# Expert rows turned in 32x32 blocks by VectorE instead of whole by TensorE, and the memory attention's value product with its operands swapped

## What is computed

```python
def memory_attention(q, mem, g_mem, w_kv):          # 4 heads of 64, 256 memory rows for each sequence
    ...
    p = jax.nn.softmax(scores, axis=-1)
    o = jnp.einsum('bhsm,bmhd->bshd', p, v)
...
def expert_choice(xn, w_router, w_gate, w_up, w_down):
    aff = jax.nn.softmax((xt @ w_router), axis=-1)   # 16 experts
    g, idx = lax.top_k(aff.T, cap)                   # each expert takes 256 + 128 rows
    xe = xt[idx]
    hdn = silu(einsum('ecd,edf->ecf', xe, w_gate)) * einsum('ecd,edf->ecf', xe, w_up)
    ye = einsum('ecf,efd->ecd', hdn, w_down) * g[..., None]
    y = zeros_like(xt).at[idx.reshape(-1)].add(ye.reshape(-1, D))
...
    o = concat([rmsnorm(o_a), rmsnorm(o_b), rmsnorm(o_c)])   # o_c is the memory attention's
    x = x + o @ w_out
    x = x + expert_choice(rmsnorm(x, g_ffn), ...)
    return rmsnorm(x, g_final)
```

## Time and profile before

| | |
|---|---|
| median of 3 runs | 3428.23 us (3425.49 to 3431.06) |
| the profiled execution | 3429.16 us |
| its span, first to last instruction | 3427.4 us |
| TensorE busy | 3269.1 us, 95% |
| VectorE, ScalarE, GpSimd busy | 1618.2, 1440.3, 543.9 us |
| mean granted TensorE clock | 0.973 |

### The profile page before, as it was taken

How to read it: one execution, slowest core, us unless ns; L and a number is a source line. 1 busy time by engine, 2 the same in 40 slices (tenths; PEclk the granted TensorE clock), 3 DMA queues, 4 the chain that set the end, 5 groups by cost and what they waited for, 6 DMA issues and landing times. The chain is left out here.

```text
span 3427.4 us, 56721 instructions
## 1 busy us (share of the span) xinstructions
PE 3269.1 (95%) x21980; PEld 2961.3 (86%) x21980; DVE 1618.2 (47%) x3498; ACT 1440.3 (42%) x3082; POOL 543.9 (16%) x543
## 2 busy tenths in 40 slices
PE   7999999997999987999489999999999999999997
PEld 5888888886777766888389999999999999999997
DVE  5445444543677765555543333333333333333454
ACT  4333333333888873333333333333333333333443
POOL 0111111112212112222101100111101111001232
PEclk9999999998999998999589999999999999999999
DMA  6111111114744444554245544555445555445785
GB/s 210 54 57 48 47 57 56 47 51 139 241 117 116 127 114 151 190 194 171 86 154 160 153 124 154 160 160 160 138 135 160 159 160 160 123 154 158 221 271 199
DMA packets 337565, 474.59 MB, mean 138 GB/s; under 512 B 22992, under 2 KB 250064, under 8 KB 337232
## 3 DMA queue, kind: packets, MB, share of 16 engines
q1 hardware_dynamic: 318784, 403.72, 36.8%
q0 software_dynamic: 18576, 68.03, 7.2%
HBM read 360.26 MB, written 111.41 MB: 138 GB/s over the span
## 5 line engine op out<-in xcount | busy, mean ns | idle before, releaser
L2041 DVE TENSOR_TENSOR warm_lo<-warm_stage,warm_hi 128x2048 fp32r<-128x2048 f32 x192 | 440.0, 2292 | 628.2 <-ACT warm_hi L1524 621.1
L1524 ACT ACTIVATE warm_hi<-warm_stage 128x2048 fp32r<-128x2048 f32 x192 | 366.5, 1909 | 0.0
L2149 PE MATMUL exp_ps_g<-exp_xT_hi,warm_lo 128*128 128x384 f32 x1024 | 346.1, 338 | 1.7 <-DVE exp_xT_lo L2048 1.7
L2149 PE MATMUL exp_ps_u<-exp_xT_hi,warm_lo 128*128 128x384 f32 x1024 | 346.0, 338 | 0.0
L2149 PE MATMUL exp_ps_u<-exp_xT_lo,warm_hi 128*128 128x384 f32 x1024 | 345.9, 338 | 0.0
L2149 PE MATMUL exp_ps_g<-exp_xT_lo,warm_hi 128*128 128x384 f32 x1024 | 345.8, 338 | 0.0
L2149 PE MATMUL exp_ps_u<-exp_xT_hi,warm_hi 128*128 128x384 f32 x1024 | 345.8, 338 | 0.0
L2149 PE MATMUL exp_ps_g<-exp_xT_hi,warm_hi 128*128 128x384 f32 x1024 | 345.8, 338 | 0.0
L1002 ACT ACTIVATE att_prob<-att_prob,att_o 128x256 f32<-128x256 f32 (+1 forms) x576 | 265.9, 465 | 73.8 <-DVE att_o L1046 70.8
L1926 POOL DMA_INDIRECT scratch_y<-exp_ye,route_slots x45 | 98.5, 2190 | 1188.6 <-ACT exp_ye L2015 1179.2
L1999 ACT ACTIVATE exp_hT_hi<-exp_hid 128x768 fp32r<-128x768 f32 x64 | 54.2, 847 | 427.7 <-DVE exp_hid L2062 427.7
(11 more groups left out here) (326 smaller groups left out, 7787.8 us busy)
## 6 DMA issues: line engine op xcount, KB each, us to landing
warm_stage<-in_w_gate SPq DMA_DIRECT2D x128, 512.0 KB, 4.5
warm_stage<-in_w_up SPq DMA_DIRECT2D x128, 512.0 KB, 4.6
warm_stage<-in_w_down SPq DMA_DIRECT2D x128, 512.0 KB, 4.5
mix_o<-scratch_o SPq DMA_DIRECT2D x72, 264.0 KB, 3.0
att_v<-scratch_v SPq DMA_DIRECT2D x64, 256.0 KB, 4.1
scratch_xn<-mix_xn SPq DMA_DIRECT2D x24, 520.0 KB, 3.2
memory_x<-in_x SPq DMA_DIRECT2D x24, 512.0 KB, 3.4
att_v<-scratch_v SPq DMA_DIRECT2D x192, 64.0 KB, 2.1
```

What stands on the lines that cost most here:

```text
L1524: self.nc.scalar.activation(self.hi[:, m % self.RW, :, :], self.stage[:, m % self.RS, :, :], ACT.Copy).then_inc(self.hi_sb, 1)
L2041: nc.vector.tensor_tensor(w_lo[:, m % RW, :, :], stage[:, m % RS, :, :], w_hi[:, m % RW, :, :].bitcast(F32), ALU.subtract).then_inc(s["w_l ...
L2149: x_ = nc.tensor.matmul(ps[:, f, 0:S], a[:, m % RW, k, f * P:(f + 1) * P], b[:, k, :], start=(n == 0), stop=(n == 3 * KC - 1))
```

## The change

Three things are changed.

**Rows for the experts.** A row of `scratch_xn` now consists of four quarters, each 256 features and its own copy of the 16 router weights (272 numbers, 1088 for a row). For experts 1 to 15 the rows are gathered a quarter at a time, by 12 indirect DMAs: slot `a` of the buffer takes, on partitions of quarter `b`, the quarter `b` of the row that belongs there, so that a transpose of 32x32 blocks within each group of 32 partitions leaves features on the partitions. `turn_quads` does this on DVE, six times for an expert, from SBUF to SBUF into `act_g` and `hid`, which nobody uses at that time; ACT (`hi_quads`) and DVE (`lo_quads`) then make the two parts. PE has no transposes left in the loop, and neither the wait on `xT_lo` ahead of the unit m = 11. Expert 0 is gathered and transposed as before. A small product ahead of the loop (`spread_rows`) works out which quarter each partition takes.

**Weights.** The features now come in another order over partitions and chunks, so `w_gate` and `w_up` are loaded in the same order: four DMAs of 256 KB for a unit, each to 32 partitions. `w_down`, and expert 0, are also loaded in four, to all partitions.

**Memory values.** The values are stationary (64 columns, two heads side by side) and the probabilities moving (128 columns). The product comes out transposed; ACT copies it (`ocT_sb`), and PE transposes it back with two transposes (`back`) in the next tile, behind `turn_k`. The chain that closes a tile is now run in the next tile, in `out_c`, `mean_bc`, `root_bc` and `out_bc`: on ACT ahead of the squares of `z_uv`, on DVE around `mean_x`.

```diff
 project_phase, ScalarE
+                def out_bc(t):
+                    act.wait_ge(s["oc_sb"], t + 1)
...
+                    nc.scalar.activation(uv_a[:, 0:D_C], oc[:], ACT.Square, accum_out=ssc).then_inc(s["sq_c"], 1)
+                    act.wait_ge(s["rs_bc"], t + 1)
...
                         if more:
                             square_x(t + 1, 1 - u, n)
+                        if not is_first(t):
+                            out_bc(t - 1)
                         act.wait_ge(s["z_uv"], t + 1)
...
+                        act.wait_ge(s["pv_ps"], t + 1)
+                        nc.scalar.activation(qcT[:], ps_o[:, 0:D_C].rearrange("p (j c) -> p j c", c=P), ACT.Copy).then_inc(s["ocT_sb"], 1)
 project_phase, TensorE
+                def back(t):
+                    pe.wait_ge(s["ocT_sb"], t + 1)
+                    for j in range(2):
+                        x_ = nc.tensor.transpose(ps_o[:, j * P:(j + 1) * P], qcT[:, j, :], ident[:])
...
-                        for h in range(HC):
+                        for j in range(HC // 2):
                             for c in range(2):
-                                x_ = nc.tensor.matmul(ps_o[:, h * HD:(h + 1) * HD], probT[:, 2 * h + c, :],
-                                                      vm[:, seq, c, h * HD:(h + 1) * HD], start=(c == 0), stop=(c == 1))
+                                for f in range(2):
+                                    h = 2 * j + f
+                                    x_ = nc.tensor.matmul(ps_o[f * HD:(f + 1) * HD, j * P:(j + 1) * P], vm[:, seq, c, h * HD:(h + 1) * HD],
+                                                          probT[:, 2 * h + c, :], start=(c == 0), stop=(c == 1))
 Weights.load, SyncE
-        for half in (1, 0):
...
+        for b in range(QUADS):
+            if w == "w_down" or e == 0:
+                k = b * KC // QUADS
...
+            else:
+                to_b, src_b = to[b * QR:(b + 1) * QR, :, :], src[:, b * QD:(b + 1) * QD, :].rearrange("o (k p) c -> p (o k) c", p=QR)
+            sp.dma_start(to_b, src_b).then_inc(self.loaded[m % self.RS], 16)
 expert_phase, GpSimd
+                def gather(e):
+                    quarters = A["xn"].rearrange("t (b c) -> (t b) c", c=Q_COLS)
+                    for j in range(ST):
+                        for a in range(QUADS):
+                            at = j * NE + e
+                            nc.gpsimd.indirect_dma_start(xe[:, e % 2, j, a * Q_COLS:(a + 1) * Q_COLS], None, quarters,
+                                                         bass.IndirectOffsetOnAxis(ap=rows_of[:, a, at:at + 1], axis=0))\
+                                .then_inc(gathered[e % 2], 16)
 expert_phase, VectorE
+                def turn_quads(e, r):
+                    j, k = r // 2, r % 2 * P
...
+                    nc.vector.transpose(turned[r % 2], by_quads(xe[:, e % 2, j, :])[:, :, k:k + P]).then_inc(s["quads_turned"], 1)
+
+                def lo_quads(e, r):
                     dve.wait_ge(s["xT_hi_sb"], e * ROUNDS + r + 1)
...
                             elif w == "w_down" and more:
-                                for r in WITHIN[m].values():
-                                    lo_x(e + 1, r)
+                                for r in WITHIN[m]:
+                                    turn_quads(e + 1, r)
+                                for r in WITHIN[m]:
+                                    lo_quads(e + 1, r)
 expert_phase, TensorE
-                                if j == NU - 1 and more:
-                                    pe.wait_ge(s["xT_lo_sb"], ROUNDS * (e + 2))
...
-                                    if more and k in WITHIN[m]:
-                                        turn(e + 1, 1 - u, i + 1 + u, WITHIN[m][k])
```

More of the change, by code:

```diff
@@ L60 @@
 GELU_C = 2.0 * (2.0 / np.pi) ** 0.5
-PICK_WIDTHS = dict(same=P, below=P, slots=2 * P, lane=4, slot=2, middle=1, bases=3 * NE, start=2, steps=2 * BITS, caps=2, level=1)
+PICK_WIDTHS = dict(same=P, below=P, slots=2 * P, lane=4, slot=2, middle=1, bases=3 * NE, start=2, steps=2 * BITS, caps=2, level=1, quad=1)
 PICK = {n: (sum(list(PICK_WIDTHS.values())[:i]), w) for i, (n, w) in enumerate(PICK_WIDTHS.items())}
@@ L654, in body @@
                             turn_k(t - 1)
+                            back(t - 1)
                         ge(pe, s["v_sb"], t)
@@ L705, in _ @@
                 turn_k(NT - 1)
+                back(NT - 1)
 SUBQ = tuple(s // 16 for s in SEQS)
@@ L1805, in _, with expert_phase @@
                                      start=True, stop=True).then_inc(s["expert_ps"], 1)
-def expert_phase(nc, A, slots, weights):
+def expert_phase(nc, A, slots, weights, table):
     S = ST * P
@@ L1978, in _, with hi_quads, hi_x @@
             def _(act):
-                def hi_x(e, r, bank=ps_t[:]):
-                    act.wait_ge(s["xT_ps"], e * ROUNDS + r + 1)
+                def hi_quads(e, r):
+                    act.wait_ge(s["quads_turned"], (e - 1) * ROUNDS + r + 1)
+                    act.wait_ge(s["unit_done"], (e - 1) * M + 2 * NU)
+                    nc.scalar.activation(tokens_of(xT_hi, r), turned[r % 2].rearrange("p (a k t) -> p a k t", a=QUADS, t=QR), ACT.Copy)\
+                        .then_inc(s["xT_hi_sb"], 1)
+                def hi_x(r, bank):
+                    act.wait_ge(s["xT_ps"], r + 1)
                     j, k = r // 2, r % 2 * 4
@@ L2101, in _ @@
                 dve.wait_ge(s["half_set"], 1)
+                nc.vector.tensor_copy(slots_f[:], slots[:].rearrange("p j e -> p (j e)")).then_inc(s["slots_f_set"], 1)
+                for a in range(QUADS):
+                    own = ident[:, a * QR:(a + 1) * QR].rearrange("p (one t) -> p one t", one=1)
+                    nc.vector.tensor_copy(lanes[:, a, :, :], own.broadcast_to([P, QUADS, QR])).then_inc(s["lanes_set"], 1)
                 split(0, 0)
+                dve.wait_ge(s["rows_ps"], 1)
+                at, _ = PICK["quad"]
+                nc.vector.tensor_scalar(rows_of[:].rearrange("p a n -> p (a n)"), ps_g[:, 0, 0:QUADS * ST * NE], float(QUADS),
+                                        table.pick[:, at:at + 1], ALU.mult, ALU.add).then_inc(s["rows_set"], 1)
                 for r in range(ROUNDS):
-                    lo_x(0, r, first_banks[r % len(first_banks)])
+                    lo_x(r, first_banks[r % len(first_banks)])
                 for m in range(1, RW - 1):
@@ L2118, in _, with spread_rows, turn @@
             def _(pe):
[L2120 removed]
+                def spread_rows():
+                    pe.wait_ge(s["slots_f_set"], 1)
+                    pe.wait_ge(s["lanes_set"], QUADS)
+                    for a in range(QUADS):
+                        x_ = nc.tensor.matmul(ps_g[:, 0, a * ST * NE:(a + 1) * ST * NE], lanes[:, a, :, :].rearrange("p b t -> p (b t)"), slots_f[:], start=True, stop=True)
+                    x_.then_inc(s["rows_ps"], 1)
+                def turn(r):
                     if r == 0:
[L2122 to L2123 removed]
+                        pe.wait_ge(gathered[0], gathers(0))
+                    ge(pe, s["xT_lo_sb"], r - len(first_banks) + 1)
                     j, k0 = r // 2, r % 2 * 4
                     for k in range(4):
[L2126 removed]
+                        c = (k0 + k) * P + (k0 + k) // 2 * NE
+                        x_ = nc.tensor.transpose(first_banks[r % len(first_banks)][:, k, :], xe[:, 0, j, c:c + P], ident[:])
                     x_.then_inc(s["xT_ps"], 1)
@@ L2211, in build @@
             if upto >= 5:
-                expert_phase(nc, A, slots, weights)
+                expert_phase(nc, A, slots, weights, table)
 def pick_constants():
```

155 lines of the change are left out of this document (100 added, 55 removed).

## The result

The changed kernel takes 3374.9 us (median of four runs, 3373.4 to 3380.9) against 3427.6 of the kernel before: a ratio of 0.985, 95% interval 0.984 to 0.986. The profiled execution took 3375.5 us, with a span of 3373.7. The forecast of 3375 holds, but its terms do not all hold.

What follows compares the result with a forecast made beforehand. PE's instruction stream was taken to set the time in every stage touched. From 3429.16 us, -37.8 (experts 0 to 13), -6.3 (expert 14), -11.5 (memory values) and +1.0 gave 3374.6, forecast as 3375; 8-in-10 range 3366 to 3391.

Steps and rivals of the forecast that it cites:

- What bounds the kernel: PE's instruction stream sets the time in every stage touched; an edit is worth what it takes from PE's stream or waits.
- Transposes: Taking them off PE saves 2.7 us in each of experts 0 to 13, 37.8 us, and 6.3 us in expert 14.
- The period of 101.76: An ordinary expert without transposes: eight units of 8.44 us plus four of 8.56, against a period of 104.50.
- Expert 15: Has no transposes already, 102.0 us to its last product; forecast to change by 0.
- the first rival: DMA or POOL's queue late in experts 14 and 15: costs 3.6 us and up to 9 more, 3378 to 3388; chance 0.13.
- the weights' ring: Loading gate and up weights four units, 34 us, ahead hides loads that take twice as long a byte.
- The rule on ports: Partitions 0 to 31 reach 8 of 16 ports: loads 1.74 times as long, up to 9 us in expert 14.
- Rival 3: Weight loads to 32 partitions at a quarter of the rate become the bound, about 3810 us; chance 0.04.
- figure of 3440 us: Total time if weight pieces to 32 partitions took 3 times as long; loads were said to decide from 2.9 times.
- Memory values: In the projection, swapped products save 0.68 us a tile, transposes back cost 0.18 to 0.22: net 0.48, 11.5 us over 24 tiles.
- Rival 2: The moved closing chain makes PE wait in the projection: the 11.5 us are lost, 3386 us; chance 0.10.
- Cover on DVE and POOL: Block transposes of about 0.7 us on DVE and 12 gathers an expert on POOL stay hidden in idle time.

Runs made afterwards that it cites:

- e3: Kernel before with the expert loop's transposes and the copies of their results left out, experts 1 to 15 using expert 0's rows; 3385.8 us, ratio 0.988.
- e5: Kernel before with 1152 unused bytes a partition between the gathered rows and the transposed ones; 3415.4 us, ratio 0.997.
- e10: Changed kernel with three small tiles (384 bytes) placed ahead of the transposed rows; 3385.4 us, ratio 0.988.
- e11: Changed kernel with 128 unused bytes ahead of the transposed rows; 3386.5 us, ratio 0.988.
- e4: Changed kernel with all weight units loaded by four 256 KB DMAs to all 128 partitions, in the old order; 3365.3 us, ratio 0.981.
- e7: Changed kernel with expert 15's last-norm tiles started one to two units later and the squares of expert 14's rows one unit later; 3366.3 us, ratio 0.983.
- e2: Kernel before with an unused 32-byte tile a partition ahead of the weights, moving all expert tiles on; 3430.0 us, ratio 1.001.
- e9: Changed kernel with expert 15's last norm started later and three small tiles (384 bytes) moved ahead of the transposed hidden values; 3362.9 us, ratio 0.981.
- e6: Changed kernel with gate and up weights loaded in matching order by eight 128 KB DMAs a unit, each to all 128 partitions; 3682.5 us, ratio 1.075.

## Why the prediction came out right

*What bounds the kernel*: right. PE's stream set the time, and what left it came back as time.

*Transposes*: right. e3 measures the 2.74 of the period, and the 101.76 of the sum of units, without any other part of the change. Expert 14 lost its wait on `xT_lo` and runs like any other.

*The period of 101.76*: wrong by 0.65 us an expert, some 9 us over experts 0 to 13. The step that failed is the silent one in "8 x 8.44 + 4 x 8.56": it took the durations of products that the change doesn't touch as kept. Their instructions are the same, but `exp_xe` grew by 1152 bytes and so moved their operands. e5 shows the effect without the change, e10 and e11 take it away within it.

*Expert 15*: wrong by 9 us. It is the first rival, in another place: DMA was late in the last pair. The working asked whether the weights' ring lasts, and it does in expert 14 even at a share of 1.01. What it missed is that the loads of the last norm and the scatter share those engines, and that weights and norm stand in one queue on SP and on ACT, and scatter and norm on POOL. e4 shows the cause (whole pieces, no wait) and e7 the path (same pieces, other order, no wait). The price in this trace was 8.2 us and 1.8 of a slower clock, within the rival's "3.6 us and up to 9 more".

*The rule on ports*: the Trainium skill, "SBUF — State Buffer", section on door 1, gave an estimate of 1.74 times; e4 against the changed kernel gives 1.57 of engine time. The direction agrees and the size is smaller here. It did decide the last pair. Rival 3 stayed away, since the point from which it decides was 2.9. Its figure of 3440 us at three times does not follow from its own sum: 26.1 + 3 x 26.2 = 104.7 us an expert gives 3429 + 15 x 0.2 - 11 = 3421.

*Memory values*: the mechanism was right and the term too large, 0.48 us a tile against 0.33. The products and `back` were priced well; two neighbours, `turn_k` and `z_v`, each hold 0.09 us more, and the working had allowed 0.04 for one. Rival 2 did not come: ACT kept 1.65 us.

*Cover on DVE and POOL*: right; e4, with all of it in place, has no wait. The estimate from "VectorE: DVE Perf Modes" of the Trainium skill, 1.24 us for a block transpose, was too high: 0.70 and 0.67 us.

So the mechanism of the transposes and its size were right, but that the sum met 3375 to the microsecond was luck. It came out because -9.3 us in experts 0 to 13 and -0.7 in expert 14, nearly all of it addresses, and -3.6 of scatter between the traces stood against +9.3 and +1.5 in and behind expert 15 and +3.8 in the projection.

## What to carry to other kernels

A sum over parts can be right by cancellation: compare stage by stage, also where the total agrees. When an edit changes the size of any tile, durations of untouched products are not safe to carry over; read them again, and try a few unused bytes. Where transfers get dearer per byte, look first at the stretch with the highest DMA share, and there at the queues in which weights stand behind something that waits.

## What the runs showed of the hardware

*Product times depend on addresses.* With the transposed rows (the moving operand) at 128 or 384 bytes past a multiple of 512 from the weights (e11; before, e2, e3, e10), 48 products of 384 columns take 8.45 us; at a multiple of 512 (after, e4, e5, e7) 8.32. The products with the hidden values as stationary operand go the other way: 8.55 at 128 or 384, 8.64 at a multiple. e9 has the two at different residues and the better time of each. Since 128 and 384 behave alike, the residue may be that of 256. Distance and place were not separated. Worked out from the sizes of the tiles and counted, modulo 256, from where the weights start in the kernel before, the fast rows lie at 0 (e5) and 32 (after), the slow ones at 128 (before) and 160 (e2, e10, e11): the place of the rows alone fits as well. Why a read depends on it is open.

*Pieces to 32 partitions* took an estimated 1.57 times the engine time of pieces to 128, at equal packets and bytes (e4 against the changed kernel).

*A DMA whose source begins with a dimension of four* ran at 92 GB/s with 0.27 of the engines busy (e6), and held up SP's queue, although its packets were cheap.
